# A two-layer transformer step on one core: an order of waits changed in eight places, collections of attention output split

## The reference

```python
def first_block(x, ...):
    xn = rms_norm(x, norm_gain)
    qa, ka, va, za, qi, ki, wi, qb, kb, vb, zb = split(xn @ w_in)
    a_out = dsa_attention(qa, ka, va, qi, ki, wi, bias_a)     # top-128 keys by an index score, softmax, 8 heads
    b_out = dilated_attention(qb, kb, vb, bias_b)             # windows of 128, 512, 2048 at dilation 1, 4, 16, 8 heads
    mixed = concat([a_out * silu(za), b_out * silu(zb)])
    return x + mixed @ w_out

def second_block(x, ...):
    q, kv, g_attn, u_pool, g_merge = split(rms_norm_2(x) @ w_in)
    a = nsa_attention(q, kv, g_attn) @ w_branch_attn          # o = g0*compressed + g1*selected + g2*window
    b = pool_mixer(u_pool) @ w_branch_pool
    ga, gb = split(sigmoid(g_merge))
    x = x + (ga * a + gb * b) @ w_out
    h = rms_norm_2(x)
    x = x + square(relu(h @ w_ff1)) @ w_ff2
    return rms_norm_2(x, norm_final)
```

## Time and profile before

| what | value |
|---|---|
| median of 3 runs | 1015.14 us (1015.06 to 1015.5) |
| the profiled execution's own time | 1015.04 us |
| its span, first to last instruction | 1013.2 us |
| mean granted TensorE clock | 0.999 |
| PE busy | 999.0 us (99%), 5134 matmuls |
| DVE, ACT, POOL busy | 704.0, 567.3, 443.4 us (69, 56, 44%) |
| chain that ended last | PE 88%, DVE 6%, ACT 2% |

### The profile page before, as it was taken

The page is one execution under the profiler, slowest core; times in us unless marked ns, Lnnn a source line. Parts: engine busy times, 40 slices in busy tenths (PEclk is TensorE's granted clock), DMA queues, the critical chain, the costliest instruction groups (busy, mean ns, idle before and its releaser), DMA issues.

```text
span 1013.2 us, 14351 instructions
## 1 busy us (share of the span) xinstructions
PE 999.0 (99%) x5134; PEld 821.2 (81%) x5134; DVE 704.0 (69%) x1235; ACT 567.3 (56%) x1034; POOL 443.4 (44%) x435
## 2 busy tenths in 40 slices
PE   9999999999999999999999999999999999999997
PEld 7788878778778898888887788888888888888886
DVE  5578898788985356824567789994232325999997
ACT  8455444777872355545577884644344346554565
POOL 0023012666737302900155430008679875774563
PEclk9999999999999999999999999999999999999999
DMA  9533321336254784233200328548999952443552
GB/s 340 106 99 94 104 63 43 84 76 191 68 216 170 238 275 136 55 83 84 61 3 1 99 91 273 183 169 293 337 355 342 358 180 65 155 144 137 207 188 83
DMA packets 109543, 158.31 MB, mean 156 GB/s; under 512 B 7024, under 2 KB 69232, under 8 KB 109472
## 3 DMA queue, kind: packets, MB, share of 16 engines
q1 hardware_dynamic: 96176, 142.81, 43.2%
q10 hardware_dynamic: 12768, 12.88, 4.0%
q0 software_dynamic: 528, 1.70, 1.0%
HBM read 131.55 MB, written 25.82 MB: 155 GB/s over the span
## 4 chain that ended last, share of the span: by engine, by line
PE 88%; DVE 6%; ACT 2%; issue 1%; DMA 1%; SPq 1%; POOL 0%; ACTq 0%; DVEq 0%
PE bank L1084 59%; PE bank L1626 5%; PE bank L1627 5%; PE bank L1628 5%; PE bank L1479 2%; PE bank L1266 2%; PE bank L1488 2%; PE bank L1237 2%; PE bank L1502 2%; DVE x L2483 1%; PE bank L1250 1%; DMA arena<-in_rel_bias 1%; DVE stats L2482 1%; DVE u_lo L2360 1%; PE bank L1389 1%
## 5 line engine op out<-in xcount | busy, mean ns | idle before, releaser
L2972 DVE TENSOR_TENSOR w_lo<-wring,w_hi 128x1024 fp32r<-128x1024 f32 x32 | 50.4, 1576 | 107.4 <-ACT w_hi L2203 107.2
L2360 DVE TENSOR_TENSOR u_lo<-wring,u_hi 128x1024 fp32r<-128x1024 f32 (+2 forms) x69 | 83.3, 1215 | 53.2 <-ACT u_hi L1803 52.7
L1084 PE MATMUL bank<-u_hi,h_hi 128*128 128x512 f32 (+1 forms) x288 | 110.9, 385 | 0.1
L1084 PE MATMUL bank<-u_hi,h_lo 128*128 128x512 f32 (+1 forms) x288 | 109.3, 379 | 0.0
L1084 PE MATMUL bank<-u_lo,h_hi 128*128 128x512 f32 (+1 forms) x288 | 109.0, 378 | 0.0
L1803 ACT ACTIVATE u_hi<-wring 128x1024 fp32r<-128x1024 f32 (+2 forms) x66 | 66.6, 1009 | 71.0 <-PE bank L1084 54.1
L1084 PE MATMUL bank<-h_hi,w_hi 128*128 128x512 f32 (+1 forms) x272 | 102.7, 378 | 0.9 <-DVE h_lo L2401 0.9
L1084 PE MATMUL bank<-h_hi,w_lo 128*128 128x512 f32 (+1 forms) x272 | 102.3, 376 | 0.0
L1084 PE MATMUL bank<-h_lo,w_hi 128*128 128x512 f32 (+1 forms) x272 | 102.1, 377 | 0.0
L1084 PE MATMUL bank<-h_hi,u_hi 128*128 128x512 f32 x224 | 93.5, 417 | 0.4 <-ACT arena L1742 0.2
L1084 PE MATMUL bank<-h_hi,u_lo 128*128 128x512 f32 x224 | 88.2, 394 | 0.0
(11 more groups left out here) (447 smaller groups left out, 2648.8 us busy)
## 6 DMA issues: line engine op xcount, KB each, us to landing
wring<-in_w_in SPq DMA_DIRECT2D x60, 512.0 KB, 3.9
wring<-in_w_ff ACTq DMA_DIRECT2D x12, 1024.0 KB, 8.6
wring<-sums_kept SPq DMA_DIRECT2D x16, 768.0 KB, 4.2
wring<-in_w_ff SPq DMA_DIRECT2D x22, 512.0 KB, 6.5
wring<-in_w_ff SPq DMA_DIRECT2D x32, 256.0 KB, 3.4
sums_kept<-wring SPq DMA_DIRECT2D x22, 256.0 KB, 5.0
arena<-in_w_out SPq DMA_DIRECT2D x16, 256.0 KB, 3.9
sets_kept<-arena SPq DMA_DIRECT2D x8, 512.0 KB, 4.4
```

The lines of the kernel that those rows point to most:

```text
L1084: last = mm(b, lhs, rhs, start=(start and n == 0), stop=(stop and n == 2))
L2360: done = v.tensor_tensor(u_lo[raw_place(u)][:, cols], raw_unit(u)[:, cols], u_hi[hi_place(u)][:, cols].bitcast(F32), ALU.subtract)
L2972: v.tensor_tensor(cut(w_lo[ring3(m)]), src, cut(w_hi[ring3(m)]).bitcast(F32), ALU.subtract).then_inc(w_lo_done, 1)
```

## The change

It has six parts, none of which adds or takes away arithmetic:

1. `value1(t // 8 - 1, 0, 0)` comes between the two turn1 of loops 8, 16, 24 and 32.
2. LOW1: the two low halves of unit F0 + 7 in loops 52 and 53, of the same pass, instead of 50 and 52. WO_HIGH: piece 2 in step 51 instead of 49; DVE's low half of that piece, which is made in the loop behind, moves with it.
3. `per_slot["qa"]`: the second slot has 2 rounds and the third 3.
4. The first two ff tiles for tokens 256 to 511: tile 0's terms 0 and 2 of chunks 0 to 3, then its term 0 of chunks 4 to 7, ahead of the wait for the last low halves; then the rest.
5. `late_scores`: in the second attention's loops t = 4, 8, ..., 28 DVE takes the reciprocal ahead of score2(t), not behind it.
6. `collect2` is called for one side at a time for the groups 0 to 5: side 0 in loop 8o + 18 and side 1 in loop 8o + 20, both behind score2(t+1), instead of both at the end of loop 8o + 16. Groups 6 and 7 are collected as before.

```diff
--- before.py
+++ after.py
@@ -202,7 +202,7 @@
     F0 = unit_of[("zb", 0)]
     HIGH1 = {filled[tile] + 2: unit_of[tile] + 2 for tile in FILL1 if unit_of[tile] + 2 < U2}
     LOW1 = {4: (F0 + 1, 0), 6: (F0 + 1, 1), 12: (F0 + 2, 0), 14: (F0 + 2, 1), 22: (F0 + 3, 0), 24: (F0 + 3, 1), 30: (F0 + 4, 0), 32: (F0 + 4, 1),
-            38: (F0 + 5, None), 44: (F0 + 6, None), 50: (F0 + 7, 0), 52: (F0 + 7, 1)}
+            38: (F0 + 5, None), 44: (F0 + 6, None), 52: (F0 + 7, 0), 53: (F0 + 7, 1)}
     GATE_AT = {tile: max(filled[tile], HALF + 8) if tile[0] == "za" else filled[tile] for tile in FILL1}
     GATE_AT["za", 2] = 54
 
@@ -212,7 +212,7 @@
     MIX_AT = {18: 0, 32: 1, 34: 2, 40: 3, 50: 4, 56: 5, 64: 6}
     MIX_LOW_AT = {22: 0, 36: 1, 42: 2, 46: 3, 54: 4, 62: 5}
     WO = [(0, 0, 2), (0, 2, 2), (0, 4, 1), (0, 5, 1), (0, 6, 1), (0, 7, 1)] + [(1, k, 1) for k in (4, 5, 6, 7, 0, 1, 2, 3)]
-    WO_HIGH = {46: 0, 47: 1, 49: 2, 53: 3, 54: 4, 57: 5, 58: 6, 64: 7}
+    WO_HIGH = {46: 0, 47: 1, 51: 2, 53: 3, 54: 4, 57: 5, 58: 6, 64: 7}
     WO_POOL = {59: 5, 63: 6}
     MIXED = [4, 5, 6, 7, 0, 1, 2, 3]
     ROW_AT = {60: ((0, 0), (0, 1)), 62: ((0, 2),), 64: ((0, 3), (0, 4)), 66: ((0, 5),), 68: ((1, 0),)}
@@ -1315,9 +1315,12 @@
                     row1(n, j)
                 if 4 <= t < NS + 4:
                     turn1(t - 4)
+                    if ahead:
+                        value1(t // NH - 1, 0, 0)
                     turn1(t - 3)
                 if t >= 8 and t % NH == 0:
-                    value1(t // NH - 1, 0, 0)
+                    if not ahead:
+                        value1(t // NH - 1, 0, 0)
                     value1(t // NH - 1, 0, 1)
                 if t >= 12 and t % NH == 4:
                     value1((t - 12) // NH, 1, 0)
@@ -1607,9 +1610,13 @@
             ff_tile(1, 0, 2 * P, range(6))
             h3(3)
             ff_tile(1, 0, 2 * P, range(6, KC))
+            for c in range(2):
+                pe.wait_ge(h_hi_done, halves("h3", NT - 1, c) + 1)
+                ff_tile(0, 2 * P, S, range(4 * c, 4 * c + 4), (0, 2) if c == 0 else (0,))
             pe.wait_ge(h_lo_done, halves("h3", NT - 1, 1) + 1)
-            for c in range(2):
-                ff_tile(c, 2 * P, S).then_inc(a_full, 1)
+            ff_tile(0, 2 * P, S, range(KC), (1,))
+            ff_tile(0, 2 * P, S, range(4, KC), (2,)).then_inc(a_full, 1)
+            ff_tile(1, 2 * P, S).then_inc(a_full, 1)
             pe.wait_ge(r_free, out2_added(NT - 1))
             for c in range(2, NF):
                 a_bank(("ff", c))
@@ -2482,7 +2489,7 @@
                     step(v.max(top8, score_of[i]))
                     step(v.match_replace(score_of[i], top8, score_of[i], TAKEN))
 
-            per_slot = {"qb": (1, 2, 2, 2), "vb": (3, 3, 3, 3), "ka": (3, 4, 3, 2), "qa": (3, 3, 2, 1), "va": (2, 2, 2, 2)}
+            per_slot = {"qb": (1, 2, 2, 2), "vb": (3, 3, 3, 3), "ka": (3, 4, 3, 2), "qa": (3, 2, 3, 1), "va": (2, 2, 2, 2)}
             assert sum(sum(n) for n in per_slot.values()) == ROUNDS
             for g, done in zip(HEADED[1:], ("kb", "qb", None, "ka", "qa")):
                 counts = per_slot[g]
@@ -2801,13 +2808,14 @@
                 v.tensor_tensor(part(pt_lo), bank[4 + k % 2][:, 0:blocks * P].rearrange("p (j s) -> p j s", s=P),
                                 part(pt_hi).bitcast(F32), ALU.subtract).then_inc(t_free, 1)
 
-            def collect2(o):
+            def collect2(o, sides=range(2)):
                 i, g = o // G2, o % G2
-                dve.wait_ge(lo_rows_done, GROUPS + o + 1)
-                if o >= 1:
-                    dve.wait_ge(attn_done, o)
+                if 0 in sides:
+                    dve.wait_ge(lo_rows_done, GROUPS + o + 1)
+                    if o >= 1:
+                        dve.wait_ge(attn_done, o)
                 cut = lambda a, r: a.rearrange("p (m r s) -> p m r s", m=2, r=2)[:, :, r, :]
-                for r in range(2):
+                for r in sides:
                     v.tensor_tensor(turned[r * HD:(r + 1) * HD, :].rearrange("p (m s) -> p m s", m=2), cut(bank[6 + o % 2][0:HD, :], r),
                                     cut(lo_rows, r), ALU.add).then_inc((turned_done, o_free)[r], 1)
                 if o < NS // NH - 1:
@@ -2849,17 +2857,22 @@
                 v.tensor_tensor(g[:, e, :], g[:, e, :], bank[(R + at) % 4][:, :], ALU.mult).then_inc(r_free, 1)
 
             for t in range(0, NS + 10, 2):
-                if t < NS:
+                late_scores = 0 < t < NS and steps2[t][0] <= 1 and t % 4 == 0
+                if t < NS and not late_scores:
                     score2(t)
                 if 2 <= t < NS + 2:
                     dve.wait_ge(e_done, NS + t)
                     v.reciprocal(den2[:, t - 2:t], den2[:, t - 2:t]).then_inc(rden_done, 1)
+                if late_scores:
+                    score2(t)
                 if t < NS:
                     score2(t + 1)
+                if 18 <= t < NS and t % NH in (2, 4):
+                    collect2((t - 18) // NH, (t % NH // 2 - 1,))
                 if 4 <= t < NS + 4:
                     prob_low(t - 4)
                     prob_low(t - 3)
-                if t >= 16 and t % NH == 0:
+                if t >= NS and t % NH == 0:
                     collect2((t - 16) // NH)
                 if t == NS + 2:
                     for i in range(NT - 1):
```

## The result

| | us |
|---|---|
| changed kernel, median of 6 runs | 1037.56 (1032.58 to 1038.08) |
| kernel before, beside it, median of 6 | 1014.8 (1014.39 to 1015.5) |
| ratio, 95% interval | 1.0209 (1.0194 to 1.0225) |
| the profiled execution, and its span | 1038.08, 1036.3 |
| mean granted clock of the span, before and now | 0.999, 0.987 |

The change makes the kernel slower by 2.1%, some 23 us, where 1.4% was forecast with an upper end of 1033.5 us. The runs of the changed kernel also lie further apart than those of before: two of six at 1032.6 with a mean clock of 0.994, four at 1037.2 to 1038.1 with 0.987 or 0.988.

The account below looks back on a forecast made before the run. TensorE, busy 999.0 of 1013.2 us at full clock, was taken as the bound. 1015.04 + 15.8 of waits - 0.5 - 0.6 - 0.9 = 1028.8, with 0.1 for the median 1028.9 us; range 1022.5 to 1033.5.

Parts of the forecast that it names:

- The size of the waits: Second attention, transposes waiting for POOL's scale at groups 0 to 5: 2.0 to 3.5 us each, 15.8 us together.
- the one on the clock: TensorE behind the six new waits: granted clock stays at full speed, so the sum adds nothing for it.
- a rival with a chance of 0.06: Clock falls to 1.2 GHz behind each new wait, for as much work as the wait: another 15.8 us, 1044.6; chance 0.06.
- The sign that I had named for being wrong: Prediction wrong if granted clock falls below full in slices 21 to 24, or no transpose wait exceeds 1 us.
- the part with fewer or shorter falls: Milder form of the clock rival, behind the six new waits: from 1034 us; the whole rival had chance 0.06.
- Loop 16 of the first attention: Value products moved ahead of the second step fill 0.5 of TensorE's 0.7 us scale wait; gain 0.5, between 0 and 0.7.
- The tables: Last gate unit's low half and output weight piece 2 moved: low-probabilities wait goes; gain 0.6, bounds 0 and 1.0 us.
- ff tiles: First two ff tiles: matmuls moved ahead fill TensorE's 0.9 us wait for last h_lo; gain 0.9, between 0.5 and 1.0.
- Round of qa: Head product comes ahead of a round, but block sums at 147.67 don't move; gain 0, up to 0.6 us.
- Hidden: Rival at the second attention's collections: POOL's wait is hidden, only gains are left; 1013.0 us, at best 1012; chance 0.06.
- partly hidden: Rival at the collections: second scale and group 0's low half hidden, DVE runs further ahead; 1020 to 1024 us; chance 0.10.
- Gains and losses cancel: Rival for the whole kernel: time unchanged within 0.2% (2 us), needing waits of only 0.3 us per group; chance 0.03.

Follow-up runs that it names:

- needless-matmul kernel: Changed kernel plus 63 needless matmuls of 512 columns, 7 to 16 ahead of each of the six waits for POOL's scale: 1029.65 us.
- group 3 alone: Changed kernel with only group 3 collected side by side in loops 42 and 44, the other groups as before: 1016.28 us, median of ten runs.

## Why the prediction was wrong, by its own steps

**The sign, the place and the mechanism held.** The forecast was slower with 0.91, by six new waits of the transposes for POOL's scale because add_turned waits for a side that comes behind pair2 of the loop. All six are there, of 1.6 to 3.8 us, and the kernel with add_turned moved on POOL shows that this order is the cause.

**The size of the waits held.** 15.8 us were forecast. The list has 14.7 for the first scales of the pairs; with the second scales the needless-matmul kernel measures 16.8, of which some 0.5 is its own matmuls beyond the wait. By group, the first was put at 3.0 and the last at 3.5; they measured 3.04 and 3.80 for the first scale alone. The last was short mainly because TensorE comes to it sooner: ahead of the scores of loop 60 it had a wait for DVE in the kernel before, which is gone in the changed one. That row of the kernel before:

```profile
581.69 0.50 PE L1479 MATMUL bank<-kT_hi,q2T_hi 64*128 64x512 f32 x2 [0.51 <-DVE stats L2838]
```

This half microsecond is in the 3.80, but it is no new loss.

**The step that failed is the one on the clock.** The sum put its cost at nothing. I had it as a rival with a chance of 0.06 and outside the range, on the ground that no row of the kernel before shows a fall. The sign that I had named for being wrong came true: the granted clock is under full in slices 21 and 23. The trace before has no wait of TensorE longer than 1.0 us in its list, so it could not speak on waits of 1.6 to 3.8. That absence should have counted as no evidence. The Trainium skill (TensorE: Matmul & The Clock Gate, section Part 1: The HAM clock gate) has that an idle TensorE falls to 1.2 GHz and is back at 2.4 only after sustained work. The measured rows agree: 0.50 behind all six waits. My full price for it was too high, on the other side: "as much work as the wait was long", another 15.8 us, where the clock cost 7.9 us by the median and 2.9 in the fastest runs. Of that rival, the part with fewer or shorter falls, from 1034, holds the measured time. With 1028.8 and this 7.9 the sum is 1036.7, within 0.9 us of the 1037.56 measured. The cost of a fall does not follow the length of its wait: the stretches give 3.4 us at the lower level behind waits of 1.6 us and of 3.8 us alike, and 6.8 behind the first, of 3.0.

**The gains.** Three terms of the sum and the round put at nothing, read as how much earlier a matmul starts in the changed kernel than the same one of before:
- Loop 16 of the first attention, forecast 0.5: the wait is 0.2 where it was 0.7.
- The tables, forecast 0.6: the wait ahead of the transposes of loop 52 is gone (1.0 before), a wait of 0.2 for the low half (L2367) and some tenths behind it have come, as the term said. Net 0.6.
- ff tiles, forecast 0.9: the wait is gone from the list; TensorE gains 1.1 us there.
- Round of qa, forecast 0: the head product starts about 0.8 us sooner, and at 149 us TensorE waits 1.1 us behind the sums, so the matmuls behind it have gained nothing. The kernel without this part is as fast.

Together with part 5 they are 1.9 us by the medians (1014.75 - 1012.85, the kernel with part 6 undone), and 2.0 had been forecast. That the two agree so closely is in part luck: the runs of either kernel spread over 1 us, and the term for the tiles was 0.2 too low.

**The rivals.** "Hidden" and "partly hidden" fall with the rows above. Moving add_turned makes the first true: it came out at 1012.67, where that rival said 1013.0. "Gains and losses cancel" is what the kernel with both sides in loop 8o + 18 does, at 1014.91.

## What to carry to other kernels

Before work is made later on one engine, look at the in-order queue of the engine that waits for it: the price is not paid by the late work but by what stands behind the wait, here the scales, and moving the wait itself behind them cost nothing. On a kernel whose TensorE is 99% busy, a new idle as long as those here (1.6 us was the shortest with a fall behind it) should be priced twice, once for its length and once for the clock that may fall behind it, with the range open to both. A trace without such an idle says nothing on whether the clock would fall.

## What the runs showed of the hardware that was not expected

- Behind a wait of TensorE of 1.6 us the granted clock fell to 0.50 in the profiled execution, and the ten executions of the same kernel are two tight groups in time and mean clock, six at 1016.25 to 1016.91 us (0.997 or 0.998) and four at 1014.27 to 1014.37 us (0.999 or 1.000). With waits of at most 1.3 us (both sides in loop 18) no run of ten shows a clock under 0.998 or a time over 1015.2.
- Needless matmuls in six waits made the kernel faster, 1029.65 against 1037.56 us, though the first wait ended at the same time and three of the others up to 0.2 us later than they had to.
- In the changed kernel the wait of 3.04 us was followed by about 6.8 us at the lower level and that of 3.8 us by about 3.4. What decides between them these runs leave open; when the fall comes differs too, as the 0.85 between 523 and 524 shows it inside the wait, while in group 3 alone it comes 1.4 us behind its end, with TensorE at work.
